# Transposes behind their own x, the state's decay on GpSimd, and half of the turned heads as transposes, in the recurrent heads of a decoder layer

## The reference, cut to what matters

```python
def wkv7_step(S, inp):
    r, d, k, v, a, b = inp
    sa = jnp.einsum('bhij,bhj->bhi', S, a)
    S = S * d[:, :, None, :] + sa[..., None] * b[:, :, None, :] + v[..., None] * k[:, :, None, :]
    return S, jnp.einsum('bhij,bhj->bhi', S, r)
```

## Time and profile before

| | us |
|---|---|
| runs of the kernel before, median of 3 | 2429.77 (2428.03 to 2432.69) |
| the profiled execution's own time | 2435.63 |
| its span | 2433.8 |
| the loop of eight passes, from its first mask to the sample chunk's | 1245.67 to 1439.60 |
| first pass; mean of the seven others | 20.1; 24.8 |

### The profile page before, as it was taken

How to read it: one execution, slowest core, us unless ns; L and a number is a source line. 1 busy time by engine, 2 the same in 40 slices (tenths; PEclk the granted TensorE clock), 3 DMA queues, 4 the chain that set the end, 5 groups by cost and what they waited for, 6 DMA issues and landing times. The chain is left out here.

```text
span 2433.8 us, 48885 instructions
## 1 busy us (share of the span) xinstructions
PE 2333.9 (96%) x20774; PEld 2201.5 (90%) x20774; DVE 1068.7 (44%) x2383; ACT 414.1 (17%) x972; POOL 518.9 (21%) x257
## 2 busy tenths in 40 slices
PE   7999999999999989999978888999999999999997
PEld 5899999999999989888556765989999999999997
DVE  4634444334444365434564554256333444433344
ACT  4100000000000142434532242140000000000003
POOL 3312121212112032101240025313121212112111
PEclk9999999999999999989799998999999999999999
DMA  9233221111011042100220002322111011111101
GB/s 342 87 104 100 73 87 52 51 36 51 18 52 52 33 120 68 36 18 27 87 91 4 5 12 93 97 88 70 53 34 52 27 42 52 52 52 34 52 9 74
DMA packets 162804, 151.11 MB, mean 62 GB/s; under 512 B 21616, under 2 KB 142113, under 8 KB 162264
## 3 DMA queue, kind: packets, MB, share of 16 engines
q1 hardware_dynamic: 162136, 146.75, 19.3%
q10 hardware_dynamic: 144, 2.23, 0.2%
q0 software_dynamic: 384, 0.07, 0.0%
HBM read 137.98 MB, written 11.34 MB: 61 GB/s over the span
## 5 line engine op out<-in xcount | busy, mean ns | idle before, releaser
L517 PE MATMUL banks<-hh,f_up_hi 128*128 128x352 f32 (+1 forms) x2064 | 675.7, 327 | 2.4 <-DVE hl L472 1.9
L519 PE MATMUL banks<-hh,f_up_lo 128*128 128x352 f32 (+1 forms) x2064 | 673.3, 326 | 0.0
L518 PE MATMUL banks<-hl,f_up_hi 128*128 128x352 f32 (+1 forms) x2064 | 672.7, 326 | 0.0
L1300 DVE TENSOR_TENSOR f_prod<-f_silu,banks 128x384 f32<-128x384 f32 x132 | 70.2, 532 | 748.8 <-PE banks L519 748.8
L517 PEld LDWEIGHTS banks<-hh,f_up_hi 128*128 128x128 f32 x2064 | 387.5, 188 | 8.2 <-issue 8.1
L532 DVE SCALAR_TENSOR_TENSOR x<-banks,mods,x 128x352 f32<-128x352 f32 (+2 forms) x544 | 306.1, 572 | 199.5 <-PE banks L519 186.0
L518 PEld LDWEIGHTS banks<-hl,f_up_hi 128*128 128x128 f32 x2064 | 388.7, 188 | 0.0
L519 PEld LDWEIGHTS banks<-hh,f_up_lo 128*128 128x128 f32 x2064 | 387.2, 188 | 0.0
L999 POOL TENSOR_TENSOR f_up_lo<-f_up_raw,f_up_hi 128x2048 fp32r<-128x2048 f32 x43 | 198.7, 4620 | 757.3 <-DVE f_up_hi L1287 757.3
L517 PE MATMUL banks<-f_a_hi,f_dn_hi 128*128 128x352 f32 (+1 forms) x1056 | 346.3, 328 | 0.9 <-DVE f_scratch L535 0.8
L519 PE MATMUL banks<-f_a_hi,f_dn_lo 128*128 128x352 f32 (+1 forms) x1056 | 344.4, 326 | 0.0
(11 more groups left out here) (375 smaller groups left out, 2764.1 us busy)
## 6 DMA issues: line engine op xcount, KB each, us to landing
f_up_raw<-in_ffn_w_gu SPq DMA_DIRECT2D x88, 512.0 KB, 5.0
f_dn_raw<-in_ffn_w_down SPq DMA_DIRECT2D x22, 1024.0 KB, 7.6
late<-in_w_ada SPq DMA_DIRECT2D x12, 1024.0 KB, 4.9
ada<-in_w_ada SPq DMA_DIRECT2D x16, 512.0 KB, 10.8
w_in_raw<-in_w_in SPq DMA_DIRECT2D x16, 512.0 KB
gates<-in_w_ada SPq DMA_DIRECT2D x8, 1024.0 KB, 6.8
x_in<-in_x_prompt SPq DMA_DIRECT2D x8, 512.0 KB, 8.5
ada<-in_w_ada SPq DMA_DIRECT2D x4, 1024.0 KB, 7.8
```

The source lines that it names most:

```text
L517: pe.matmul(out, wh, rh, start=(n == 0), stop=False)
L518: pe.matmul(out, wh, rl, start=False, stop=False)
L519: ins = pe.matmul(out, wl, rh, start=False, stop=(n == last))
L1300: dve.tensor_tensor(prod[u % 2][:, 0:n], silu[u % 2][:, 0:n], k.psum[2 * (u % 2) + 1][:, 0:n], ALU.mult).then_inc(up_free, 1)
```

## The change

Four things change. The transposes of a stream stand directly behind its own x (`turn_step(s0)` ahead of `x_step(s1)`). Pieces of the serial part move: value_w(q) ahead of t of level 2 and seq_w(q) between the two t; seq_u(q) ahead of t of level 4; seq_o(q) from the end of level 8 to level 16, behind the transposes; value_w(c0) ahead of and seq_w(c0) between the t of level 16. `t_free` waits, ahead of these, until ACT has copied the transposes of both streams. In `turns` the order of products changes, and a head that lands on the lower half (`to == 0`) is turned by `pe.transpose` of 64x64. DVE adds to the state, GpSimd multiplies by the decay, and DVE's adds move: c0 - 2 ahead of level 2's x, c1 - 2 behind level 8's t. The bonus products on GpSimd follow the decays of odd chunks. ACT's list keeps its order.

```diff
+            def decayed(c):
+                pool.wait_ge(state_added, c + 1)
+                pool.tensor_tensor(state[:], state[:], k.p_end[:, :, c:c + 1].broadcast_to([P, PAIRS, HD]), ALU.mult
+                                   ).then_inc(state_done, 1)
+            for c in range(NCHUNK - 1):
+                decayed(c)
+                m = c // 2
+                if c % 2 and m < PAIRS:
+                    pool.tensor_tensor(k.bon[:, m], k.bon[:, m], k.u[:, 8 + m], ALU.mult).then_inc(bonus_full, 1)
...
+            def turned_head(out, of, m, r, to):
+                into, src, eye_r = out[HALVES[to], m], of[HALVES[r], m], ident[HALVES[r], HALVES[r]]
+                if to == 0:
+                    return pe.transpose(into, src, eye_r)
+                return pe.matmul(into, src, eye_r, start=True, stop=True)
...
-                heads_both(pe, (half(st.bank[0], 0), a_of(c), b_of(c), True, True), (half(st.bank[1], 0), v_of(c), eye, True, True, None))
-                heads_both(pe, (half(st.bank[0], 1), b_of(c), eye, True, True), (half(st.bank[1], 1), k_of(c), eye, True, True, st.pe)).then_inc(st.pe, 1)
+                for m in range(PAIRS):
+                    for r in HALVES:
+                        pe.matmul(gram[r, m], a[r, m], b[r, m], start=m == 0, stop=m == PAIRS - 1)
+                    for r in range(2):
+                        turned_head(v_out, v_of(c), m, r, 1 - r)
+                for m in range(PAIRS):
+                    for r in range(2):
+                        b_last = turned_head(b_out, b, m, r, r)
+                    for r in range(2):
+                        k_last = turned_head(k_out, k_of(c), m, r, 1 - r)
...
                     x_step(s0, c0, m)
-                    x_step(s1, c1, m)
...
                     turn_step(s0)
+                    x_step(s1, c1, m)
                     turn_step(s1)
                     if i and m == 2:
                         seq_o(p)
+                        t_free(s0, c0, m)
+                        t_free(s1, c1, m)
+                        value_w(q)
                     if i and m == 4:
                         read_of_state(q)
+                        t_free(s0, c0, m)
+                        t_free(s1, c1, m)
+                        seq_u(q)
                     if i and m == 8:
                         seq_s(q)
+                    if m == 16:
+                        if i:
+                            seq_o(q)
+                        t_free(s0, c0, m)
+                        t_free(s1, c1, m)
+                        value_w(c0)
                     if m == 32:
                         read_of_state(c0)
                     t_step(s0, c0, m)
+                    if i and m == 2:
+                        seq_w(q)
+                    if m == 16:
+                        seq_w(c0)
                     t_step(s1, c1, m)
-                    if i and m == 2:
-                        value_w(q)
-                        seq_w(q)
-                    if i and m == 4:
-                        seq_u(q)
-                    if i and m == 8:
-                        seq_o(q)
-                    if m == 16:
-                        value_w(c0)
-                        seq_w(c0)
...
             def new_state(c):
                 dve.wait_ge(seq_pe, count(SEQ_PE, c, "s"))
-                dve.tensor_tensor(state[:], state[:], s_ps, ALU.add)
-                dve.drain()
-                dve.tensor_tensor(state[:], state[:], k.p_end[:, :, c:c + 1].broadcast_to([P, PAIRS, HD]), ALU.mult
-                                  ).then_inc(state_done, 1)
+                if c:
+                    dve.wait_ge(state_done, c)
+                dve.tensor_tensor(state[:], state[:], s_ps, ALU.add).then_inc(state_added, 1)
```

More of the change, by code:

```diff
@@ L2465, in rwkv_heads @@
     NE = NP_TOK // HD
-    seq_pe, seq_act, state_done, state_zero = (k.sem(n) for n in ("seq_pe_steps", "seq_act_steps", "state_done", "state_zero"))
+    seq_pe, seq_act, state_done, state_zero, state_added = (
+        k.sem(n) for n in ("seq_pe_steps", "seq_act_steps", "state_done", "state_zero", "state_added"))
     w_begun, o_begun, o_valued, s_begun = (k.sem(f"seq_{n}") for n in ("w_begun", "o_begun", "o_valued", "s_begun"))
@@ L2550, in _ @@
             ins.then_inc(ends_done, 1)
-            for m in range(PAIRS):
-                pool.wait_ge(state_done, 2 * m + 1)
-                pool.tensor_tensor(k.bon[:, m], k.bon[:, m], k.u[:, 8 + m], ALU.mult).then_inc(bonus_full, 1)
+            def decayed(c):
[7 more added lines that the diff above has]
+                    pool.tensor_tensor(k.bon[:, m], k.bon[:, m], k.u[:, 8 + m], ALU.mult).then_inc(bonus_full, 1)
             pool.wait_ge(streams[0].pe, count(LOCAL_PE, NI, "tok"))
@@ L2562, in _ @@
             ins.then_inc(pad_done, 1)
+            decayed(NCHUNK - 1)
             for m in range(PAIRS):
@@ L2629, in turns @@
                 pe.wait_ge(st.dve, count(LOCAL_DVE, n, "mask_k"))
-                heads_both(pe, (half(st.bank[0], 0), a_of(c), b_of(c), True, True), (half(st.bank[1], 0), v_of(c), eye, True, True, None))
-                heads_both(pe, (half(st.bank[0], 1), b_of(c), eye, True, True), (half(st.bank[1], 1), k_of(c), eye, True, True, st.pe)).then_inc(st.pe, 1)
+                a, b = a_of(c), b_of(c)
+                gram, b_out, v_out, k_out = (half(bank, n) for bank in st.bank for n in range(2))
+                for m in range(PAIRS):
[8 more added lines that the diff above has]
+                        k_last = turned_head(k_out, k_of(c), m, r, 1 - r)
+                    if m == PAIRS - 1:
+                        b_last.then_inc(st.pe, 1)
+                        k_last.then_inc(st.pe, 1)
             def x_step(st, c, m):
@@ L2645, in turn_step, with t_free @@
                 ins.then_inc(st.pe, 1)
+            def t_free(st, c, m):
+                pe.wait_ge(st.turned, TURNS * (c // 2) + LOCAL_LEVELS.index(m) + 1)
             def t_step(st, c, m):
                 pe.wait_ge(st.dve, count(LOCAL_DVE, c // 2, f"x{m}"))
-                pe.wait_ge(st.turned, TURNS * (c // 2) + LOCAL_LEVELS.index(m) + 1)
+                t_free(st, c, m)
                 if f"t{m}" == last_step(c):
@@ L3034, in _ @@
                 level1(s1, c1)
+                if i:
+                    new_state(c0 - 2)
                 for m in LOCAL_LEVELS:
@@ L3037, in _ @@
                     x_step(s1, c1, m)
[L3038 to L3041, removed]
                     t_step(s0, c0, m)
                     t_step(s1, c1, m)
+                    if i and m == 8:
+                        new_state(c1 - 2)
             st, c = streams[0], SAMPLE_CHUNK
```

## The result

The changed kernel takes 2475.7 us (median; 2468.23 to 2480.08), 1.0175 times the kernel before, 95% interval 1.0153 to 1.0198. By the medians that is 46 us slower than the 2429.8 before (1.9%; the ratio above is the one of the comparison), outside the range of 2422 to 2444. One execution of ten of the experiment on the decay took 3250 us and is left out of its figures.

The account below looks back on a forecast made before the run. Chains of waits, with PE stopping for instruction blocks, were taken to set the loop's pace. Levels +13.5 us over seven passes, less 11.0 us of relief, turns and decay 0: +2.5 us, so 2432 us, range 2422 to 2444.

Parts of the forecast that it names:

- I take 0: Turns: small transposes in place of products leave a chunk's 0.95 us as it is, 0 us.
- The upper bound: Turns: 0.15 us for each change between matmul and transpose, 8 changes in 16 chunks, 19 us more.
- R3: Turns: small transposes cost a change each way, +19 us on the forecast, 2451; chance 0.05.
- R4: Passes: turns' transposes and the longer wait lower the clock in six more passes, +5.5 us, 2437.5; chance 0.05.
- level 16: Level 16 of a pass: seq_o's copy on ACT delays the tt copies and value_w, loss 1.15 us.
- Level 4: Level 4 of a pass: seq_u ahead of t waits for both tt copies, loss 0.69 us.
- level 8: Level 8 of a pass: only the reordered transposes count, 0.21 us more.
- The ACT queue: Level 16: the copy of seq_o's result stands ahead of both tt copies on ACT; 1.15 us a pass lost.
- The decay: State's decay multiply on GpSimd: 0.63 us later, hidden by the waits for tt; 4.4 us in seven passes if uncovered.
- The sum for all but the turns: Seven passes: 13.5 us lost in the levels less 11.0 us of relief, +2.5 us; turns taken as 0.
- The relief: PE's issue waits in the loop: 11.0 us fewer from shorter records and vanished stops; bounds 0 and 17.3.
- R1: Loop: instruction fetch gets ahead, all 17.3 us of stops go, turns 2.9 us faster; -6.7 us, 2423; chance 0.27.

Follow-up runs that it names:

- the experiment on the decay: The kernel before with only the decay of the state on GpSimd, DVE's adds where they stood: 2430.6 us, 1.0005.
- the 64 waits: The kernel before with 64 more PE waits in each of seven passes, for a count long reached: 2445.8 us, 1.0068.
- the kernel without small transposes: The changed kernel with products with the identity again in place of the 64x64 transposes, all else kept: 2432.5 us, 1.0014.

## Why the prediction was wrong

The step that failed is the one on the turns, "I take 0". I had a row for its price: between x and the 128-wide transposes PE lost 0.16 us at a change (0.40 less 0.24) and as much on the way back. I wrote that this prices a change of tile and that here the tile stays. The runs show that the change between product and transpose is enough: 0.15 and 0.17 us at 64x64 too, and turns of 3.5 us where I kept 0.95. The upper bound and R3 stood on the right mechanism and were still halved, since 8 counted the runs of transposes and each has two changes: 8 x 2 x 0.16 x 16 = 41 us, where the turns show (3.5 - 0.98) x 16 = 40. R3 with its chance of 0.05 was the true case, and with both ways counted it would have said 2473. That this lies 3 us from the time is in part luck, since R3 has neither the clock nor the stops.

The traces close the sum for the loop. It takes 245.6 us in the changed kernel and 201.6 without the small transposes, 44.0 apart: 40 us of turns at full clock, 7 of the clock in the second turns (below), 6.5 of the clock in the first pass (11.5 us longer, 5 of them its turns), less 10.3 us of stops.

The Trainium skill had two sentences that should have moved this chance. TensorEngine Tiling (Array Packing), "Tiling Modes" says that changing the tiling mode drains TensorE, and "Restrictions" there that column tiling disables the transpose mode for fp32. If a 64x64 fp32 transpose is therefore no column tile, products and transposes are of two modes, and each change drains. The gaps agree with that, but the profile names the same tile, 64*64, for transposes (L2631) and products (L2632), and that this is the reason no run here shows.

R4 came true beside it, in part. In four of the seven second turns of the changed kernel the clock is at 0.50, at 1.2 GHz, behind a first stretch of turns in which PE starts new records only every 0.1 to 0.2 us, two or three together; they take 5.17 us against 3.47, 1.7 more each, or 7 us. With the new turns alone six of seven passes have such a stretch; with four runs of transposes or fewer none of the turns in the seven passes has it. The first pass, which the prediction took as unchanged, is at 0.50 for most of its length in all of them, and in the changed kernel the clock costs more there, 6.5 us, than the turns, 5.0. That the transposes and not the gaps between them do it was not separated; with the 64 waits the clock fell at gaps alone, but at gaps of 3 us.

Point by point, most of the rest was right. With the stops taken out and over seven passes, level 16 went from 3.32 to 4.55 us, 1.23 more (forecast 1.15). Level 4 went from 3.11 to 3.52, 0.4 more (0.69), and level 8 stayed at 3.0 (0.21). So the levels after were well worked and the chain still somewhat too dear, as level 4 before was longer than the working's 2.71. The ACT queue: forecast 1.15 us a pass, measured 1.1, and 5 to 7 us in the time when it is mended. The decay: hidden.

The sum for all but the turns was +2.5 us; the kernel without small transposes is +3.1 by the medians of its comparison (2432.5 against 2429.5), with an interval from no change to +7. That the two agree is in part luck. The relief was smaller: issue fell from 18.3 to 12.0 us there, 6.3 and not 11.0. In the traces the loop is 7.7 us longer (201.6 against 193.9), which is near 13.5 less 6.3; outside the loop these two executions differ by 12 us the other way, the one before having 27 us at a clock of 0.50 ahead of it. In the changed kernel nearly all of the stops went, as in R1, but because the turns, where PE ran ahead of its instructions, became three times as long: the 43 us are what is left when these 10 are given back.

## What to carry to other kernels

Count a transpose on PE by the changes between it and products, not by its passes: each change cost 0.15 to 0.17 us here, while four passes of products start in 0.06 us. Look at the granted clock beside it, in the first pass too: here even one run of transposes a chunk went with a first pass 8 us longer, for a reason that stays open. Where products with an identity do the work, as here, leave them; if there have to be transposes, fewer and longer runs cost less. When a step is moved on one engine, read the list of the engine that copies its result: there the old order can put the copy in front of those that others wait for. And take the length of a stage before from its rows, pass by pass, not from the working alone. Last, where a row of the trace has a price for nearly the same thing, take it as the price until a row shows that the difference matters.

## What the runs showed of the hardware

- A change between 64x64 fp32 products and 64x64 fp32 transposes: 0.15 us there, 0.17 back; within a run transposes start in pairs 0.05 to 0.08 us apart.
- The first pass of the loop is at a clock of 0.50 for 24 to 31 us in all five kernels with small transposes, one run a chunk being enough, and for 3 to 7 us around its start in seven of the nine without. The reason stays open.
- Waits of PE for a count already reached took 0.05 us each (64 in 3.1 to 3.3 us), where four records of products start in 0.06. Waits added to a dense list are not free.
- PE's stops for instructions shrink when the chain gets slower and grow back when it gets faster (issue 18.3, 12.0 and 1.7 us at 24.8, 25.8 and 30.5 us a pass), so that most edits of a few tenths of a microsecond a level did not show in the time. It is not the pass's length alone: with one run of transposes, and 24 matmuls a pass fewer, a pass takes 25.6 us and issue is 3.5.
